# The Fourier transforms of the second block moved into the weave of its last recurrence heads, and the modulation of layer 1 dealt out at an even rate

## The chip, the cores and the metric

One core of one Trainium2 chip runs the whole program. The metric is the time on the device in microseconds (us), the median of several executions. Lower is better.

## The reference, cut to what matters

Two blocks run one after the other over 512 tokens of width 1024. The change touches the second block alone. It has two layers. Layer 0 also carries 256 context tokens beside the 512 (six tiles of 128 tokens), layer 1 has outputs for the 512 alone (four tiles). In each layer a projection `hl @ w_in` is cut into five pieces for a gated recurrence with four heads, q, k and v for a differential attention with four heads, and 256 columns `u` for a Fourier mix:

```python
def fourier_mix(u):
    uh = split_heads(u, FT_GROUPS).astype(jnp.float32)
    y = jnp.fft.fft2(uh, axes=(1, 3), norm="ortho").real
    return y.reshape(u.shape).astype(u.dtype)

yl = jnp.concatenate([hgrn_out(ol_f + ol_b, pl[2]), diff_out(od_l), fourier_mix(pl[8])], axis=-1) @ w_out
ml = modulation(c, w_mod[l], b_mod[l])      # silu(c) @ w_mod: 1024 x 6144, needed when layer l starts
```

The result of the Fourier mix is read only by the output projection (`@ w_out`), after the recurrence. The modulation of layer 1 is read only when layer 1 begins.

## The kernel before

The kernel is written as a plan. Python code adds steps with `P.add(kind, ...)`, and each engine's program then walks the same list and issues its own part of every step, so the order of the plan is the order of every engine's queue. Nothing is reordered on the chip. A step's waits are semaphore values that the plan has worked out. `fence()` makes all engines drain and wait for each other.

TensorE (PE) multiplies, ScalarE (ACT) and VectorE (DVE) copy out of PSUM and do the elementwise work, GpSimd (POOL) helps out, SyncE (SP) issues the loads. In this block projections that must be exact are made of three products of split halves (`SplitWeights.by_token`, `HD` high and `LT`/`LX` low halves of the activations).

The order in each layer `l` of the second block:

1. Token-major projections for q and k with weights `W1` (`tok_split`), rotary embedding, and turns into `QKT`.
2. Six tiles with weights `W2` (columns 3072 to 3584): `DV` (values of the attention) and `U` (input of the transforms), 24 matmuls for each tile.
3. A fence.
4. `rj` / `rj_d`: six additions that join high and low halves into `HT3`, three on POOL (L3240) and three on DVE (L3149). Then `swap`: four copies by POOL's DMA queue (L3244) into `QS` and `KS`, which lie over the low halves and so wait for all six additions.
5. The transforms, bare: tables `k_dft` (2 x 1 MB, both layers) and `k_dftc` (2 x 256 KB, layer 0 alone) are loaded into the two weight slots, multiplied with `U` into `PQ`, and `PQ` is multiplied with the constant `cs64` into `FTT`.
6. A fence, then `attention_stage`, into which the projections of heads 0 and 1 (`project(0)`, `project(1)`) are woven by the rate `FILL`. `project(0)` opens with a load of three weight pieces and waits for it.
7. A fence, then the recurrence. For head `h` in 0 to 3, `main(h)` has 24 lead steps in layer 0 and 16 in layer 1. Into them are woven the modulation of layer 1 (in layer 0 alone, `MODS[h]` steps for each lead step), `flow` (the projections of heads 2 and 3, `FLOW[l]` steps for each lead step: 0.64 and 0.93), and `prepare` of the next head (`RATE`). `modulation` has 24 chunks of 1 MB of weights, 32 `mod_m` matmuls each, one load slot for most of them; each group of four chunks has 32 steps, and one more step opens it, 193 in all. What is left of it after the four heads runs at the end, bare.
8. A fence, then the output projection and the feed-forward layer.

The weave is a counter: `with_some(lead, other, rate)` takes `rate` steps of `other` for each step of `lead`.

```python
for h in range(4):
    lead = main(h) if h < 3 else first_half(main(h))
    together(with_some(with_some(lead, mods, MODS[h]), flow, FLOW[l]), preps[h], RATE[l][h], 1)
```

A matmul group of the weave, `proj`, is added in two halves (`pj0`, `pj1`). With `hold=True` its copy out of PSUM is added later, by `proj_copies`.

## Time and profile before

| what | us |
|---|---|
| time, median of 3 runs | 3159.25 (3156.93 to 3161.83) |
| span of the profiled execution | 3152.5 |
| median less span | 6.8 |
| TensorE busy | 2894.6, 92% of the span |
| VectorE busy | 1617.8, 51% |
| ScalarE busy | 1033.2, 33% |
| GpSimd busy | 192.1, 6% |

The profile is of one execution, of which only the span is listed and no whole time of its own; the 6.8 us between its span and the median of the runs is taken as the part that lies around the span. "PE" is the matmul row, "PEld" its weight loads, "PEclk" the clock that was granted to TensorE as a share of 2.4 GHz. A busy time of PE at a clock under 1.00 is longer than the same work at full clock.

### The profile page before, as it was taken

Reading aid. Unit: us, or ns where it says so; the run is one execution under the profiler, and the core shown is the slowest. Engines: PE = TensorE matmul, PEld = TensorE weight load, DVE = VectorE, ACT = ScalarE, POOL = GpSimd, SP = SyncE. Lnnn points to the kernel's source line nnn. Section 1 sums busy time; section 2 is a strip of 40 time slices with the busy share of each in tenths; the row PEclk is TensorE's granted clock in tenths of the full one; section 3 lists DMA queues with packets and bytes.
Section 4 is the critical chain, followed back from the end, with each engine's and each line's share of the span. In section 5 each row is a group of like instructions: output and inputs, shape, how many; then the busy total and the mean of one; then the engine's idle time right before and its main releaser. Section 6 shows DMA issues by size and latency. Waiting matters only on the chain.

```text
span 3152.5 us, 44843 instructions
## 1 busy us (share of the span) xinstructions
PE 2894.6 (92%) x18762; PEld 2379.0 (75%) x18762; DVE 1617.8 (51%) x3363; ACT 1033.2 (33%) x2010; POOL 192.1 (6%) x240
## 2 busy tenths in 40 slices
PE   7988899999999999898799999999899897899998
PEld 6766688888976666687668888888666687578886
DVE  4333544444446355877763424333935677654444
ACT  3223333223344145344232212111415444332222
POOL 0000000000000100100000000000210245100001
PEclk9999999999999999899899999999999898999999
DMA  7434322222222210222512122121121110223231
GB/s 238 154 107 146 103 74 61 54 59 69 61 101 95 77 34 1 85 81 82 190 65 94 47 74 67 54 67 54 54 72 34 31 41 1 94 94 110 91 105 56
DMA packets 228404, 250.58 MB, mean 79 GB/s; under 512 B 5696, under 2 KB 193196, under 8 KB 226668
## 3 DMA queue, kind: packets, MB, share of 16 engines
q1 hardware_dynamic: 227296, 245.77, 24.4%
q8 instruction: 148, 2.42, 0.3%
q0 software_dynamic: 576, 1.84, 0.3%
q14 instruction: 52, 0.43, 0.0%
q10 hardware_dynamic: 332, 0.12, 0.0%
HBM read 236.43 MB, written 9.44 MB: 78 GB/s over the span
## 4 chain that ended last, share of the span: by engine, by line
PE 55%; DVE 8%; ACT 4%; issue 2%; DMA 1%; POOL 1%; POOLq 0%; SPq 0%; ACTq 0%; DVEq 0%
PE PS L2199 52%; PE PS L2203 2%; ACT AR L181 1%; ACT L176 1%; PE PS L2409 1%; DMA WR<-in_w_in 1%; DVE AR L3181 1%; ACT EX L181 1%; DVE AR L2922 0%; DVE EX L3168 0%; DVE AR L2938 0%; DMA WR<-in_w_mod 0%; ACT STAT L181 0%; POOL HT L3240 0%; DVE AR L2947 0%
## 5 line engine op out<-in xcount | busy, mean ns | idle before, releaser
L2199 PE MATMUL PS<-HI,WC 128*128 128x512 f32 (+2 forms) x1600 | 427.9, 353 | 0.6 <-DVE WC L3162 0.6
L2199 PE MATMUL PS<-AR 128*64 128x64 f32 (+7 forms) x3436 | 301.7, 269 | 63.1 <-ACT AR L181 25.0
L2199 PE MATMUL PS<-DW,DH 128*128 128x384 f32 (+1 forms) x1344 | 357.2, 348 | 0.9 <-DVE AR L2783 0.9
L181 ACT ACTIVATE AR<-PS 128x256 f32<-128x256 f32 (+4 forms) x389 | 165.8, 453 | 553.7 <-PE PS L2199 434.0
L2199 PEld LDWEIGHTS PS<-AR 128*64 128x64 f32 (+5 forms) x3436 | 253.7, 171 | 109.5 <-issue 33.8
L2199 PEld LDWEIGHTS PS<-HI,WC 128*128 128x128 f32 x1600 | 284.0, 189 | 42.5 <-DVE WC L3162 1.1
L2199 PE MATMUL PS<-LO,WC 128*128 128x512 f32 (+2 forms) x800 | 282.2, 353 | 0.0
L2199 PE MATMUL PS<-WR,HT 128*128 128x128 f32 (+2 forms) x1296 | 255.2, 355 | 11.6 <-ACT AR L181 5.8
L2199 PE MATMUL PS<-HT,WR 128*128 128x256 f32 (+1 forms) x928 | 257.2, 429 | 6.7 <-DMA WR<-in_w_in 3.1
L2199 PEld LDWEIGHTS PS<-DW,DH 128*128 128x128 f32 x1344 | 241.9, 192 | 9.7 <-issue 7.1
L2199 PEld LDWEIGHTS PS<-WR,HT 128*128 128x128 f32 x1296 | 193.9, 198 | 66.2 <-issue 41.7
L181 ACT ACTIVATE EX<-PS 128x256 f32<-128x256 f32 (+2 forms) x158 | 66.6, 430 | 513.7 <-PE PS L2199 513.7
L2199 PE MATMUL PS<-WC,AC 128*128 128x512 f32 x960 | 228.4, 395 | 0.3
L2199 PE MATMUL PS<-DW,DL 128*128 128x384 f32 (+1 forms) x672 | 227.3, 338 | 0.0
L2199 PEld LDWEIGHTS PS<-HT,WR 128*128 128x128 f32 x928 | 171.7, 190 | 69.9 <-issue 43.3
L2199 PEld LDWEIGHTS PS<-WC,AC 128*128 128x128 f32 x960 | 179.1, 189 | 44.1 <-DVE AR L3181 7.4
L2203 PE MATMUL PS<-CON,AR 128*128 128x128 f32 (+1 forms) x950 | 153.0, 287 | 56.0 <-DVE AR L3129 16.2
L3162 DVE TENSOR_TENSOR WC<-WR,WC 128x1024 fp32r<-128x1024 f32 x96 | 116.3, 1222 | 165.4 <-ACT WC L181 165.4
L181 ACT ACTIVATE WC<-WR 128x1024 fp32r<-128x1024 f32 x96 | 99.9, 1054 | 273.0 <-PE PS L2199 273.0
L2203 PEld LDWEIGHTS PS<-CON,AR 128*128 128x128 f32 (+1 forms) x950 | 117.0, 147 | 93.2 <-issue 51.4
L3168 DVE TENSOR_TENSOR EX<-EX,PS 128x512 f32<-128x512 f32 x66 | 39.2, 594 | 256.7 <-ACT EX L181 256.7
L2199 PEld LDWEIGHTS PS<-LO,WC 128*128 128x128 f32 x800 | 151.3, 189 | 20.4
(458 smaller groups left out, 4948.1 us busy)
## 6 DMA issues: line engine op xcount, KB each, us to landing
WR<-in_w_ffn_in SPq DMA_DIRECT2D x40, 1024.0 KB, 6.4
WR<-in_w_in_b SPq DMA_DIRECT2D x51, 512.0 KB, 6.0
WR<-in_w_mod SPq DMA_DIRECT2D x12, 2048.0 KB, 8.0
WR<-in_w_mod SPq DMA_DIRECT2D x24, 1024.0 KB, 5.5
WR<-in_w_ffn_out SPq DMA_DIRECT2D x22, 1024.0 KB, 4.9
WR<-in_w_in SPq DMA_DIRECT2D x40, 512.0 KB, 5.3
WR<-in_w_out SPq DMA_DIRECT2D x8, 2048.0 KB, 11.3
WR<-in_w_in SPq DMA_DIRECT2D x4, 2048.0 KB, 7.8
```

Of the source, the lines that this page charges most:

```text
L176: self.o.preload_act_table_set(need)
L181: return self.o.activation(out, in_, func, **kw)
L2199: mm = lambda o, l, r, start, stop: e.o.matmul(o, l, r, start=start, stop=stop, skip_group_check=True)
L2203: m = e.o.transpose(bk[0:a.shape[1], 128 * i:128 * i + a.shape[0]], a, ident[0:a.shape[0], 0:a.shape[0]])
L2409: m = e.o.matmul(o, q, k, start=True, stop=True)
L3162: tt(lo, src, hi.bitcast(F32), ALU.subtract).then_inc(sem("cv_d"))
L3168: tt(v, v, pu, ALU.mult).then_inc(sem("gt_m"))
L3181: tt(y, y, bk, ALU.add).then_inc(sem("dn_d"))
```

## The change

The transforms leave their place between the two projections and the attention. `U` is no longer a buffer: its tiles are written into `FTT`, where the results later replace them. A generator `transform()` does the same products and is the last link of `flow`, behind `project(3)`. It waits in the plan until head 1 has ended, since its tables and `PQ` lie in buffers of head 1 (`X`, `XC`), and copies out on ScalarE alone, one group late. The tables are loaded by `tables()`: for `k_dft` one load of 1792 KB and one of 256 KB, for `k_dftc` one of 512 KB.

The first fence goes. The additions `rj` are all on VectorE, one behind each tile of step 2, 1024 elements a partition as before. The load of `project(0)`'s first three weight pieces is issued behind tile 1 of step 2. Two steps of `project(0)` run ahead of the attention stage, whose count starts one lower. `MODS` goes from (1.4, 1.4, 2.2, 2.6) to (2, 2, 2.2, 2.2). What is left of `flow` after the heads runs at the end like the modulation.

```diff
-        RATE, FILL, MODS = ((1, 2, 2, 1), (1.4, 2.5, 2.5, 1)), ((0.45, 0.58), (0, 0.82)), (1.4, 1.4, 2.2, 2.6)
+        RATE, FILL, MODS = ((1, 2, 2, 1), (1.4, 2.5, 2.5, 1)), ((0.45, 0.58), (0, 0.82)), (2, 2, 2.2, 2.2)
...
-                both_parts = [(DV[:, i, :], 0, 256), (U[:, i, :], 256, 512)][:2 if i < nt else 1]
-                tok_split(i, W2, 512 if i < nt else 256, th, both_parts, eng_of(i))
+                o = [(DV[:, i, :], bk_cols(0, 256)), (FTT[:, :, 128 * i:128 * i + 128], bk_cols(256, 512, 2))][:2 if i < nt else 1]
+                p = tok_split(i, W2, 512 if i < nt else 256, th, o, eng_of(i))
+                cols = slice(128 * i, 128 * i + 128)
+                other = LTs[l][:, :, cols] if i < 4 else LXs[l][:, :, 128 * (i - 4):128 * (i - 4) + 128]
+                P.add("rj", HT3[:, :, cols], HDs[l][:, :, cols].bitcast(F32), other.bitcast(F32), [("pj", p.n)])
...
+                if i == 1:
+                    w = load([(128 * j, 128, w2[:, c:c + 128]) for j, c in enumerate((1536, 2048, 0))], 8, 384)
+                    first_w = [Chunk(w.slot, w.view[:, :, 128 * j:128 * j + 128], w.ready, w.until, ()) for j in range(3)]
...
-            fence()
-            for ks in (slice(0, 4), slice(4, 8)):
-                for lo, other in ((0, LTs[l][:, ks, 0:256]), (256, LTs[l][:, ks, 256:512]), (512, LXs[l][:, ks, :])):
-                    P.add("rj_d" if lo == 256 or (lo == 512 and ks.start) else "rj", HT3[:, ks, lo:lo + 256], HDs[l][:, ks, lo:lo + 256].bitcast(F32), other.bitcast(F32), need)
...
-                tabs = [load_flat(A[name][:, c * kt * n:(c + 1) * kt * n], kt * n) for c in range(2)]
-                ready = []
-                for c in range(2):
-                    v = k3(tabs[c].view, kt)
-                    for f in range(2):
-                        j, bk, until = lring.take()
-                        p = proj_now(bk[:, 0:n], [(U[:, tiles0 + k, 128 * f:128 * f + 128], v[:, k, :]) for k in range(kt)], tabs[c], [], until,
-                                     [(eng_of(f), PQ[:, c, f, 0:n], bk[:, 0:n], None)], pq_until)
...
+            def transform(ring=hturn, heads=heads, set_until=set_until, both=both, FTT=FTT):
+                while not heads[1].ended:
+                    yield
...
+                def one(n, pairs, w, need, to, free):
+                    settle()
+                    while ring.full():
+                        yield
+                    j, bk, b_until = ring.take()
+                    points = []
+                    for p in proj(bk[:, 0:n], pairs, w, need, b_until, [("a", to, bk[:, 0:n], None)], free, hold=True):
+                        if n == 512:
+                            yield
+                    owed.append((j, p, points))
+                    yield
+                    return points
...
+                w = tables("k_dft", [X[:, 0:3584], XC[:, 0:512]], until)
...
+                    for f in range(2):
+                        ready = []
+                        for c in range(2):
+                            pairs = [(FTT[:, f, off + 128 * k:off + 128 * k + 128], rows[kt * c + k]) for k in range(kt)]
+                            ready.append((yield from one(n, pairs, w, [], PQ[c][:, 0:n], free)))
+                        stage_one = (("pj", P.count["pj1"]),)
+                        settle()
+                        yield
+                        yield from one(n, [(cs64[:, 128 * c:128 * c + 128], PQ[c][:, 0:n]) for c in range(2)], None, ready[0] + ready[1],
+                                       FTT[:, f, off:off + n], ())
...
-            due = [0]
+            due = [-1]
+            for _ in range(2):
+                next(filling)
...
-            flow = itertools.chain(*[project(h, prr=hturn, slots=by_quarter, after=heads[0] if h == 3 else None) for h in (2, 3)])
+            flow = itertools.chain(*[project(h, prr=hturn, slots=by_quarter, after=heads[0] if h == 3 else None) for h in (2, 3)], transform())
...
-            for _ in mods:
+            for _ in itertools.chain(mods, flow):
                 pass
```

## Rows read from the trace of the kernel before

**Rows 1.** The page: busy time, share of the span and instructions of two engines.
```profile
PE 2894.6 (92%) x18762; PEld 2379.0 (75%) x18762; DVE 1617.8 (51%) x3363; ACT 1033.2 (33%) x2010; POOL 192.1 (6%) x240
```

**Rows 2.** Stretches: length, busy us of PE, PEld, DVE, ACT, POOL, PEclk, DMA.
```profile
1034.00:1057.00 23.00, 22.93 (x102) 18.66 (x100) 1.51 (x4) 1.35 (x5) 0.00 (x0) 1.00 0.00 1
...
1057.00:1082.80 25.80, 23.13 (x68) 11.95 (x68) 11.06 (x9) 3.57 (x8) 12.47 (x7) 1.00 0.50 137
2315.20:2336.20 21.00, 17.67 (x40) 7.44 (x40) 9.78 (x6) 2.10 (x4) 12.34 (x7) 1.00 0.77 192
```

**Rows 3.** The chain that ended last, layer 0: start us, us, what.
```profile
1049.91 7.04 PE PS L2199 x31
...
1079.07 6.39 DMA WR<-in_w_in
...
1085.51 3.70 PE PS L2199 x8
```

**Rows 4.** The same chain, layer 1.
```profile
2299.82 15.28 PE PS L2199 x90
...
2327.67 8.51 POOLq L3194
```

**Rows 5.** Matmuls of the transform of 512 tokens, layer 0: busy us, mean ns.
```profile
L2199 PE MATMUL PS<-WR,AR 128*128 128x512 f32 x32 | 14.0, 595 | 0.8 <-ACTq L2478 0.8
L2199 PE MATMUL PS<-AR,CON 128*128 128x512 f32 x8 | 3.7, 601 | 0.9 <-ACT AR L181 0.9
```

**Rows 6.** Additions on DVE, duration ns min/median/max.
```profile
L3149 DVE TENSOR_TENSOR HT<-HD,LT x4: 1226/2296/3367, 1057.7 to 2316.7; 128x1024 f32<-128x1024 f32 x4
```

**Rows 7.** The swap's issues on POOL, and POOL's drain behind them, each layer.
```profile
1068.00 2.51 POOL L3244 DMA_DIRECT2D AR<-AR  x4 [0.31 <-POOL HT L3240]
2325.88 2.38 POOL L3244 DMA_DIRECT2D AR<-AR  x4 [0.30 <-POOL HT L3240]
...
L3194 POOLq DRAIN  x1: 5895/5895/5895, 1069.3 to 1069.3; - x1
...
L3194 POOLq DRAIN  x1: 8946/8946/8946, 2327.2 to 2327.2; - x1
```

**Rows 8.** Timeline: first groups of PE behind the second fence of layer 1.
```profile
2336.22 1.26 PE L2409 MATMUL PS<-AR 32*128 32x384 f32 x8 [2.06 <-POOLq L3194]
2337.41 5.02 PE L2199 MATMUL PS<-HT,WR 128*128 128x512 f32 x8
...
2342.36 0.93 PE L2409 MATMUL PS<-AR 32*128 32x384 f32 x8
```

**Rows 9.** Timeline: the last matmuls of `project(3)` in layer 0.
```profile
1478.61 3.84 PE L2199 MATMUL PS<-WR,HT 128*128 128x128 f32 x32
```

**Rows 10.** Stretches: layer 0's recurrence in three, the end of layer 1's; columns as in 2.
```profile
1285.00:1482.00 197.00, 182.66 (x2270) 162.03 (x2271) 147.79 (x422) 77.66 (x150) 14.28 (x4) 0.97 0.30 93
1482.00:1553.00 71.00, 48.31 (x953) 40.76 (x952) 64.92 (x193) 23.27 (x46) 4.15 (x2) 0.83 0.55 178
1553.00:1573.40 20.40, 14.34 (x245) 11.09 (x245) 6.88 (x17) 3.47 (x18) 0.00 (x0) 0.83 0.38 113
...
2648.00:2704.00 56.00, 33.53 (x487) 29.55 (x485) 45.89 (x106) 18.58 (x42) 29.28 (x52) 0.79 0.21 76
```

**Rows 11.** Modulation matmuls between 1300 and 1482 us, ten chunks of 32.
```profile
L2199 PE MATMUL PS<-WR,MISC 128*2 128x128 f32 x320 | 10.6, 272 | 0.0
```

**Rows 12.** Waits from 1553 to 1573.5 us: who waited for whom, us, times, longest.
```profile
DVE AR L2962 <- ACT STAT L181: 6.0, 1, 6.0
DVE MOD L2864 <- PE PS L2203: 4.8, 2, 4.1
...
PEld PS L2199 <- DMA WR<-in_w_mod: 2.5, 1, 2.5
```

**Rows 13.** The page: loads of 2048 KB, count, size, us to landing.
```profile
WR<-in_w_mod SPq DMA_DIRECT2D x12, 2048.0 KB, 8.0
...
WR<-in_w_out SPq DMA_DIRECT2D x8, 2048.0 KB, 11.3
```

More of the change, by code:

```diff
@@ L380, in load @@
             c = Chunk(slot, v, (f"w{slot}", wloads[slot]), wuntil[slot], loads)
-            P.add("load", c)
-            return c
-        def load_flat(ap, cols):
-            slot = wturn[0] % 2
-            wturn[0] += 1
-            wloads[slot] += 16
-            c = Chunk(slot, wslots[slot][:, 0:cols], (f"w{slot}", wloads[slot]), wuntil[slot], [(wslots[slot][:, 0:cols], ap)])
             P.add("load", c)
@@ L1641, in tok_split @@
                 j, bk, until = lring.take()
-                p = proj_now(bk[:, 0:n], w.by_token(l, i, 0, n), w.ready, need, until, [(eng, o, bk[:, lo:hi], None) for o, lo, hi in to], free)
+                p = proj_now(bk[:, 0:n], w.by_token(l, i, 0, n), w.ready, need, until, [(eng, o, view(bk), None) for o, view in to], free)
                 lring.done(j, *p.done)
@@ new lines, in build @@
+                if i == 1:
+                    w = load([(128 * j, 128, w2[:, c:c + 128]) for j, c in enumerate((1536, 2048, 0))], 8, 384)
+                    first_w = [Chunk(w.slot, w.view[:, :, 128 * j:128 * j + 128], w.ready, w.until, ()) for j in range(3)]
+            th = [("rj", P.count["rj"])]
+            turned = [("qturn_" + e, turn_counts["q" + e]) for e in "ad"]
+            for a in (0, 64):
+                P.add("swap", QS[64 - a:128 - a, :, :], QKT[a:a + 64, 0:2, 0:512], th + turned)
+                P.add("swap", KS[64 - a:128 - a, :, :], QKT[a:a + 64, 2:4, 384:768], th + turned)
@@ L1885, in main, with tables, settle @@
                 yield from recur(heads[h], ended)
+            def tables(name, to, until):
+                wloads["f"] += 16 * len(to)
+                at_, loads = 0, []
+                for a in to:
+                    loads.append((a, A[name][:, at_:at_ + a.shape[1]]))
+                    at_ += a.shape[1]
+                w = Chunk("f", None, ("wf", wloads["f"]), until, loads)
+                P.add("load", w)
+                return w
+            def transform(ring=hturn, heads=heads, set_until=set_until, both=both, FTT=FTT):
+                while not heads[1].ended:
+                    yield
+                until, owed = set_until[1], []
+                def settle():
+                    if owed:
+                        j, p, points = owed.pop()
+                        proj_copies(p)
+                        ring.done(j, *p.done)
+                        points += p.done
+                def one(n, pairs, w, need, to, free):
[10 more added lines that the diff above has]
+                    return points
+                PQ, free = [XC[:, 512:1024], XC[:, 1024:1536]], until
+                w = tables("k_dft", [X[:, 0:3584], XC[:, 0:512]], until)
+                rows = [X[:, 512 * k:512 * k + 512] for k in range(7)] + [XC[:, 0:512]]
+                for name, n, off in (("k_dft", T, 0), ("k_dftc", TC, 512))[:2 if both else 1]:
+                    kt = n // 128
+                    if off:
+                        w, rows = tables(name, [X[:, 0:1024]], stage_one), [X[:, 256 * k:256 * k + 256] for k in range(4)]
+                    for f in range(2):
[8 more added lines that the diff above has]
+                                       FTT[:, f, off:off + n], ())
+                        free = (("pj", P.count["pj1"]),)
+                settle()
@@ L3244, in swap @@
                 e.o.dma_start(to, src).then_inc(sem("swap"), 16)
-            return dict(fence=fence, rj=rj, swap=swap, hp2=hp2, hl1=hl1, hl2=hl2, g2=g2, an=an, dump=dumped(e))
+            return dict(fence=fence, swap=swap, hp2=hp2, hl1=hl1, hl2=hl2, g2=g2, an=an, dump=dumped(e))
         def sp_program(e):
```

37 lines of the change are left out of this document (9 added, 28 removed).

## The prediction, as put on record before the changed kernel was run

> **What bounds the kernel now.** I read the page first. TensorE is busy for 92% of the span and VectorE for 51% [rows 1], so what is taken off TensorE's queue is worth its time wherever nothing else sets the pace, and what is moved costs its time again unless it lands in a gap. So I then asked for stretches: the place that the transforms leave, and the place that they go to.
>
> They leave a stretch of 25.8 us in layer 0 and 21.0 us in layer 1 in which TensorE is busy for 23.1 and 17.7 us [rows 2] and the chain runs over TensorE in layer 0 [rows 3]. In layer 1 it runs over POOL's queue, at the end over 8.51 us of POOL's drain, which ends after TensorE has finished the transforms [rows 4]. So the transforms of layer 1 hide most of a wait that is there without them.
>
> They go to the time behind `project(3)`. Its last group of matmuls starts at 1478.61 and ends at about 1482 in layer 0 [rows 9]; in layer 1 the place is about 2648. Up to there the recurrence of layer 0 is bound by TensorE, busy for 182.7 of 197 us [rows 10]. Behind it TensorE is idle for 22.7 of 71 us and 6.1 of 20.4 us in layer 0, 22.5 of 56 us in layer 1, and VectorE is busy for 64.9 of 71 us and 45.9 of 56 us. There is a gap for TensorE work, but VectorE is the bound beside it with only 6 us to spare in the 71.
>
> **The front, step by step.** Removed from TensorE: in both layers the 14.0 and 3.7 us of the 512 tokens [rows 5], 17.7 us, and in layer 0 those of the context too, with which it is 23.1 us [rows 2]. Today the time from the end of the last `W2` matmul to the first score of the attention is 1082.8 - 1056.95 = 25.8 us in layer 0 [rows 2, 3] and 2336.22 - 2315.10 = 21.1 us in layer 1 [rows 4, 8].
>
> What is late next is the swap. It still waits for all additions, and the fence behind it waits for POOL's drain. The additions of tiles 0 to 4 run on VectorE during step 2, where it is busy for 1.5 us in 23 [rows 2]: with that cover gone they would cost five times 1.2 us a layer, so they cost nothing. The last one is exposed. One such addition took 3.36 us beside POOL's and 1.23 us at the least [rows 6]; POOL has none in the new stage, so I take 1.2 us and keep 3.4 us as the other bound. Then 0.3 us to POOL, 2.5 us of issues, and the drain's end: 1069.3 + 5.9 = 1075.2 is 4.7 us behind the last issue's end at 1070.5 in layer 0, and 2336.1 is 7.9 us behind 2328.3 in layer 1, where three weight loads ran beside it [rows 7]. In the new order those weight loads come earlier (their slot is free when `W1` has been used, before tile 1), and the table loads are gone, so I take 4.7 us. Sum: 1.2 + 0.3 + 2.5 + 4.7, with 0.1 for semaphores, 8.8 us of idle TensorE in each layer; the bounds are 8.8 and, with both worse ends, 14.2 us. No project work can fill it, since the two early steps stand behind the fence. They are eight matmuls of 512 columns, 3.7 us as the group at 1085.51 [rows 3], moved ahead of an attention stage in which TensorE is the fullest engine, so they neither gain nor lose.
>
> The first term is 25.8 - 8.8 = 17.0 us gained in layer 0 and 21.1 - 8.8 = 12.3 us in layer 1. In layer 0 the wait for the first weight load goes too: the load landed at 1079.07 + 6.39 = 1085.46, and the next group began at 1085.51, 1.8 us after the scores of 0.93 us that began at 1082.8 [rows 3, 8]; these 1.8 us are gained. Against it, after the drain in layer 1 TensorE ran its first groups slow, 1.26 us for 0.93 and 5.02 for 3.70 [rows 8, 3]. After an idle of 8.8 us layer 0 will pay those 1.7 us as well, layer 1 pays them already. Front in all: 17.0 + 1.8 - 1.7 + 12.3 = 29.4 us gained.
>
> The Trainium skill has a rule that picks between the two ends for the addition: SBUF — State Buffer, Who interferes with whom, says that a VectorE instruction with two SBUF inputs contends with a GpSimd instruction that reads SBUF, and that the second to issue is blocked for the whole of the first. By it the 1.2 us holds once POOL adds nothing, and without it the exposed wait would be 2.2 us longer a layer, 4.4 us in the sum; the minimum beside the maximum agrees with it.
>
> **The recurrence, step by step.** Counting the yields: `project(2)` and `project(3)` take 18 each in layer 0 and 17 in layer 1, the transforms 22 and 14. At 0.64 a lead step the 36 end at lead step 57 of 96 and the 22 more at 91; at 0.93 the 34 end at step 37 of 64 and the 14 more at 52. Both fit before the loop's end, and the trace has `project(3)` end about there [rows 9].
>
> Modulation: at the new rates layer 0's heads 0 and 1 take 96 steps of it instead of 67.2. These 28.8 steps are 3.6 chunks at 10.6 / 10 = 1.06 us each [rows 11], with their turns some 4.4 us of TensorE work moved into the stretch where it is full to 93%: +4 us. Between 0 (all in its gaps) and 4.4. The three loads more that it brings forward are of 1 MB, in a stretch whose DMA share is 0.30 [rows 10], and cost nothing there.
>
> The tail: today 193 steps meet 182.4, so some eleven run bare at the end, and from 1553 to 1573.4 us TensorE waited for a modulation load, VectorE 4.8 us for a turn of it and 6.0 us for the last output behind it [rows 12]. At 24 x 8.4 = 201.6 the modulation ends four lead steps early. I take 5 us gained, between 0 and the 13.3 us that these three waits sum to.
>
> Tables: 2 MB land in 8.0 to 11.3 us [rows 13], and TensorE's first transform product stands in the plan right behind the load with no step between. SP issues it when the last modulation chunk before it has been used, up to one chunk's period earlier. A chunk is 8 of the 2.2 steps a lead step, 3.6 lead steps of some 2.3 us (71 us for 31), 8.4 us. So TensorE waits for 9.6 less an average 4.2, about 5.4 us, between 0 and 11.3; behind it every later instruction of TensorE's queue waits, the next `multiply` of head 2 among them, and VectorE behind that. Since TensorE idles a third of this stretch, I count 3 us. Modulation loads queued behind the tables come up to 10 us late with a period of 8.4: part of the same bound. In layer 1 SP has nothing before it but head 1's end, three lead steps before, and its table is asked for as soon as that is met; the first product follows it by at least those steps and part of head 2, some 10 us: nothing, up to 1 us. The second table of layer 0 is a quarter of the size and has a pair of `cs64` matmuls and a lead step to land in: nothing.
>
> The Trainium skill, DMA: Bandwidth & Descriptors, Anatomy of one DMA, fits a transfer issued from GpSimd as 2.0 us plus bytes over 436 GB/s, by which 2 MB would take 6.8 us, an estimate. By it the wait would be 2.6 us and its cost 1.5 us, the sum 1.5 us better; the table is issued from SP and modulation loads run beside it, so I stay with the rows, which are slower.
>
> The products themselves: 23.1 us in layer 0 for a gap of some 23 us between lead steps 57 and 91, to which the 4.4 us of modulation and the time at the low clock add. A granted clock of 0.83 over 71 us is 24 us at half speed; if half of them were busy, 6 us come back when the gaps are filled. That makes 33 us of room. In layer 1 17.7 us go into about 17.5 idle and 6 of clock. So TensorE will be some 85 to 90% busy next to a VectorE at 82 to 91%. Each half of a product is 1.8 us in front of the next matmul of the recurrence. Bounds: 0, if always in a wait, and 40.8, if never. The nearest row is the stretch before, where TensorE at 93% and VectorE at 75% ran side by side [rows 10]; here VectorE is fuller, and I take a quarter of the 40.8 as delay: 10 us, 6 in layer 0 and 4 in layer 1. The twelve and six copies on ScalarE of 0.4 to 0.6 us lie in a ScalarE that is busy for a third.
>
> Sum for the recurrence: 4 - 5 + 3 + 6 + 4 = 12 us lost. In all 29.4 - 12 = 17.4 us gained. The profiled span becomes 3152.5 - 17.4 = 3135.1 us, and with the 6.8 us by which the median stands above the span, 3141.9 us.
>
> **Rivals.** First, all hidden: the products and tables fall into waits, the recurrence loses 4 us or less or gains by the tail. 29.4 less 4 to plus 5 gives 3125 to 3134 us. For it speak 22.7 and 22.5 us of idle at a low clock; against it VectorE's 64.9 of 71. Second, no change: VectorE and TensorE lock step, half of the 40.8 us is exposed (20 instead of 10), the table wait costs its full 11 and the front's idle is 12 us twice (6 more); 17.4 - 10 - 8 - 6 is a loss of 7 us if all three come and a gain of up to 6 if two do: 3153 to 3165 us. For it speaks that TensorE already waits for VectorE in step and the drain took 8.9 us in layer 1. Third, slower: the one mechanism is that the products land on the recurrence's chain, each half in front of a matmul for which VectorE waits. With all 40.8 us exposed the recurrence loses 4 - 5 + 3 + 41 = 43 and the kernel is 14 us slower, about 3173; it turns slower when more than 27.4 us, two thirds of the 40.8, are exposed. Against it stands the spare unit between a multiply and its reduce in `recur`. Fourth, the move is only half made: banks of the turn ring are full, the transforms lag and some run bare behind the last head. Each step so left costs about 1 us (23.1 / 22), and with eight left the gain is 9 us, 3150: the high end of the forecast's own range.
>
> **Chances.** The forecast, 3134 to 3151 us, 0.61, the fourth rival within its upper end; all hidden 0.18; no change 0.13; slower 0.08. A measurement of this kernel can tell 0.2%, 6.3 us, from no change: faster 0.79, the same 0.12, slower 0.09. The range that leaves out no more than two in ten runs from 3128 to 3154 us.
>
> **What the profile after would show.** The front: a gap of TensorE of about 9 us in each layer, ended by POOL's drain, the additions at 1.2 us each on VectorE, and no wait for a weight load behind it. The recurrence: products of 512 columns out of `X` between `project(3)` and about three quarters of head 3; a wait of TensorE for the table in layer 0 alone; a granted clock near 1.00 where it was 0.83 and 0.79. The stretch from the stage's first matmul to the last fence 8 us longer in layer 0 and 4 us in layer 1. The prediction is wrong if POOL's drain takes more than 12 us of the front, or if VectorE's idle time behind `project(3)` grows by more than 20 us.

## The result, and the profile after

The changed kernel takes 3183.64 us (median of 4 runs, 3182.89 to 3185.59), the kernel before 3158.09 us (4 runs). The ratio is 1.0092, with an interval from 1.0076 to 1.0108: **slower, by 25.6 us between the medians, where 17 us less were forecast**. The profiled execution has a span of 3184.0 us, 31.5 us above that of before. Part of that difference is which executions were profiled: where the time of the profiled execution is listed, it lies 1.3 to 1.7 us above its span, so the one of the kernel before, with a span of 3152.5, must have taken about 3154 us, some 4 us less than its median, and the one of the changed kernel took 3185.59, 2 us more than its median. The 6.8 us that the table of before puts around the span are for the most part this.

TensorE's busy time, on the page of the profile of the changed kernel, is 13 us more than in [rows 1] for the same number of instructions:

```profile
PE 2907.9 (91%) x18762; PEld 2381.0 (75%) x18762; DVE 1609.3 (51%) x3360; ACT 1037.0 (33%) x2019; POOL 171.6 (5%) x234
```

**Where the time went.** SP's queue gives marks that every version has: the store of `x_spill`, the load of `k_mask` at the recurrence's start, and the load of `x_spill` at its end. The timeline of SP, the kernel before and then the changed one:

```profile
985.13 0.34 SPq L3269 DMA_DIRECT2D x_spill<-X  x1
...
1285.30 0.82 SPq L3269 DMA_DIRECT2D AR<-k_mask  x2
1573.34 0.34 SPq L3269 DMA_DIRECT2D X<-x_spill  x1
```

```profile
989.46 0.34 SPq L3297 DMA_DIRECT2D x_spill<-X  x1
...
1283.83 0.81 SPq L3297 DMA_DIRECT2D AR<-k_mask  x2
1604.62 0.34 SPq L3297 DMA_DIRECT2D X<-x_spill  x1
```

Differences of such marks give the stages, in us. "Front" is steps 1 and 2 and the attention, "rec" the recurrence, "other" all that lies outside these four, where the change edits nothing. Each row is of one execution. "Other" differs by up to 14 us between versions with no edit there, so I take the stages as the evidence.

| kernel | front, layer 0 | rec, layer 0 | front, layer 1 | rec, layer 1 | other | span |
|---|---|---|---|---|---|---|
| before | 300.2 | 288.0 | 239.6 | 197.8 | 2126.9 | 3152.5 |
| changed | 294.4 | 320.8 | 231.7 | 199.2 | 2138.0 | 3184.0 |
| mods_alone | 300.3 | 296.0 | 238.0 | 199.0 | 2135.2 | 3168.4 |
| mods_old | 299.0 | 308.5 | 231.8 | 199.2 | 2131.1 | 3169.5 |
| layer0_in_place | 303.5 | 287.0 | 231.6 | 199.0 | 2130.4 | 3151.6 |
| early_tables | 294.4 | 298.6 | 234.3 | 199.2 | 2133.7 | 3160.2 |
| early_old | 294.5 | 290.9 | 231.6 | 199.1 | 2132.6 | 3148.6 |
| no_transforms | 298.8 | 286.5 | 231.6 | 199.0 | 2131.4 | 3147.3 |
| early_first_mod | 298.7 | 309.4 | 231.6 | 198.9 | 2141.3 | 3179.9 |
| first_product_later | 297.1 | 312.0 | 231.5 | 199.1 | 2134.6 | 3174.2 |
| old_rates_half_step | 295.9 | 292.0 | 231.8 | 199.1 | 2135.4 | 3154.2 |
| early_old_swap_sp | 286.6 | 289.5 | 224.6 | 196.2 | 2134.2 | 3131.0 |
| before_swap_sp | 300.1 | 287.4 | 240.1 | 200.0 | 2128.9 | 3156.4 |
| changed_swap_sp | 286.6 | 314.9 | 220.5 | 199.7 | 2130.9 | 3152.5 |
| swap_sp_no_early_steps | 283.0 | 291.7 | 227.3 | 199.5 | 2133.0 | 3134.5 |
| tables_no_early_steps | 286.3 | 289.6 | 229.8 | 198.5 | 2135.2 | 3139.4 |

The changed kernel against before: fronts 5.8 and 8.0 us shorter (29.4 was the forecast for both), recurrence of layer 0 longer by 32.8 us (forecast: 8), of layer 1 by 1.4 (forecast: 4), and 11.1 us outside. So the loss is for the most part one stage: layer 0's recurrence.

How far is a stage to be trusted? In layer 1's front the versions with the same instructions there agree within 0.4 us, early_tables apart (2.6 us more). In layer 0's front they do not. From the attention's first score to the load of `k_mask`, the stretch takes 201.8 or 201.9 us in changed, early_tables and early_old, and 206.2 to 206.4 us in mods_old, no_transforms, early_first_mod, first_product_later, early_old_swap_sp and changed_swap_sp, with 203.3 in old_rates_half_step between them, though the same instructions stand in it. The granted clock takes another course: in the third and the fourth 20 us from the first score it is 0.91 and 1.00 in early_old, 0.99 and 0.84 in no_transforms. What sets the course is not shown. So a difference of up to 4.6 us in this front proves nothing, and the changed kernel's 5.8 us there were measured in the shorter course. In the recurrences the same plan comes out within 2.2 us in layer 0 (early_old, early_old_swap_sp, swap_sp_no_early_steps, tables_no_early_steps), with one exception, changed against changed_swap_sp, 5.9 us.

**The front.** Timeline of the changed kernel on VectorE, POOL and TensorE, with POOL's drain at the fence, first in layer 0, then in layer 1; these answer to [rows 3, 4, 6 to 8]:

```profile
1061.33 1.23 DVE L3181 TENSOR_TENSOR HT<-HD,LX 128x1024 f32<-128x1024 f32 x1 [3.55 <-PE PS L2231]
1063.15 2.51 POOL L3272 DMA_DIRECT2D AR<-AR  x4 [788.30 <-DVEq L2797]
L3226 POOLq DRAIN  x1: 7374/7374/7374, 1064.5 to 1064.5; - x1
1071.93 10.12 PE L2231 MATMUL PS<-HT,WR 128*128 128x512 f32 x16 [10.64 <-POOLq L3226]
1081.98 0.93 PE L2441 MATMUL PS<-AR 32*128 32x384 f32 x8
...
L3226 POOLq DRAIN  x1: 7570/7570/7570, 2349.7 to 2349.7; - x1
2357.33 9.13 PE L2231 MATMUL PS<-HT,WR 128*128 128x512 f32 x16 [10.53 <-POOLq L3226]
2366.39 0.93 PE L2441 MATMUL PS<-AR 32*128 32x384 f32 x8
```

The addition takes the 1.23 us that was forecast. The drain ends at 1064.5 + 7.4 = 1071.9, 6.2 us behind the last issue's end (1065.66), not 4.7. TensorE waits 10.6 us in each layer. Then the two early project steps run: 16 matmuls, not eight, and at a granted clock of 0.70 and 0.78 they take 10.1 and 9.1 us. The first score starts at 1081.98, 20.7 us behind the last `W2` matmul's end at 1061.3, where before it was 25.8.

**The recurrence of layer 0.** Timeline of the changed kernel, SP's queue and then TensorE's, around the two table loads:

```profile
1487.36 7.14 SPq L3292 DMA_DIRECT2D WR<-in_w_mod  x2
1494.61 0.56 SPq L3292 DMA_DIRECT2D X<-k_dft  x1
1495.21 0.43 SPq L3292 DMA_DIRECT2D XC<-k_dft  x1
...
1563.24 8.17 SPq L3292 DMA_DIRECT2D WR<-in_w_mod  x2
1571.45 0.92 SPq L3292 DMA_DIRECT2D X<-k_dftc  x1
```

```profile
1493.01 1.05 PE L2231 MATMUL PS<-WR,MISC 128*2 128x128 f32 x32
1504.36 5.52 PE L2231 MATMUL PS<-X,AR 128*128 128x512 f32 x8 [10.29 <-DMA XC<-k_dft]
...
1569.92 1.05 PE L2231 MATMUL PS<-WR,MISC 128*2 128x128 f32 x32
1577.55 3.78 PE L2231 MATMUL PS<-X,AR 128*128 128x256 f32 x8 [6.58 <-DMA X<-k_dftc]
```

Read them across. TensorE ends a modulation chunk at 1494.06; that frees the slot for which SP's second modulation load has stood waiting; SP issues it, then the table at 1494.61; and the table's product is the very next thing in TensorE's queue. The table gets no lead, and TensorE waits for its whole transfer, 10.3 us: both parts landed 9.1 us behind their issue, within the 8.0 to 11.3 us of [rows 13]. At 1571.45 the same thing happens to the small table, 6.6 us. The products that free its buffer had ended at 1554.7, so it was not they that held its load. The Trainium skill, DMA: Bandwidth & Descriptors, Anatomy of one DMA, says that a semaphore wait of a DMA happens on the issuing sequencer before dispatch; this case's trace agrees: each table was issued within 0.6 us of the end of the chunk that the load ahead of it had waited for.

**Stretches.** The changed kernel, columns as in [rows 2], with [rows 2 and 10] as the counterparts; the last line lies as far behind the load of `k_mask` of layer 1 as the last of [rows 10] does:

```profile
1061.30:1082.80 21.50, 10.87 (x24) 4.33 (x24) 1.23 (x1) 1.26 (x3) 2.51 (x4) 0.68 0.38 91
1285.00:1482.00 197.00, 179.67 (x2279) 158.47 (x2277) 143.52 (x415) 75.53 (x144) 14.28 (x4) 0.95 0.36 109
1482.00:1553.00 71.00, 54.27 (x720) 37.88 (x719) 45.66 (x124) 22.52 (x47) 4.14 (x2) 0.88 0.36 122
...
2671.80:2727.80 56.00, 46.91 (x525) 32.69 (x523) 44.52 (x103) 20.93 (x46) 29.02 (x52) 0.94 0.21 76
```

In layer 1 the products raise TensorE from 33.5 to 46.9 us busy and the clock from 0.79 to 0.94. In layer 0 VectorE, busy for 64.9 of these 71 us before, has 45.7. About half of that is the first table: VectorE's longest wait in the stretch, 10.2 us, is for a product that stands behind the table's, and with the tables early (early_tables) it is busy for 55.0 us. In that stretch of mods_alone it is busy for 58.4 and of early_old for 60.3, so the rates and the products have a part in it too. The second table's wait lies behind this stretch.

### The profile page after: what moved, and what is told of

It is laid out like the page before. It is cut to its first block, busy times and chain, and to the rows that moved or that the text cites. A ratio compares the mean times of both kernels' runs of the same rounds, so it can differ in the third digit from the quotient of the medians.

```text
span 3184.0 us, 44817 instructions
## 1 busy us (share of the span) xinstructions
PE 2907.9 (91%) x18762; PEld 2381.0 (75%) x18762; DVE 1609.3 (51%) x3360; ACT 1037.0 (33%) x2019; POOL 171.6 (5%) x234
## 4 chain that ended last, share of the span: by engine, by line
PE 55%; DVE 8%; ACT 4%; issue 2%; DMA 1%; POOLq 0%; POOL 0%; SPq 0%; DVEq 0%; ACTq 0%
PE PS L2231 52%; PE PS L2235 2%; ACT AR L181 1%; PE PS L2441 1%; ACT L176 1%; DVE AR L3213 1%; DVE STAT L3145 1%; ACT EX L181 1%; DVE EX L3200 0%; POOLq L3226 0%; DMA WR<-in_w_in 0%; ACT STAT L181 0%; DVE AR L2954 0%; DVE AR L3125 0%; DVE OBl L3194 0%
## 5 line engine op out<-in xcount | busy, mean ns | idle before, releaser
L2231 PE MATMUL PS<-AR 128*64 128x64 f32 (+7 forms) x3436 | 299.0, 264 | 52.9 <-ACT AR L181 23.6
L181 ACT ACTIVATE AR<-PS 128x512 f32<-128x512 f32 (+4 forms) x386 | 164.4, 453 | 550.9 <-PE PS L2231 413.1
L2231 PEld LDWEIGHTS PS<-HT,WR 128*128 128x128 f32 x928 | 175.3, 194 | 91.3 <-issue 46.2
L2235 PE MATMUL PS<-CON,AR 128*128 128x128 f32 (+1 forms) x950 | 155.4, 290 | 57.4 <-DVE AR L3161 17.4
```

What stands on the lines that cost most here:

```text
L181: return self.o.activation(out, in_, func, **kw)
L2231: mm = lambda o, l, r, start, stop: e.o.matmul(o, l, r, start=start, stop=stop, skip_group_check=True)
L2235: m = e.o.transpose(bk[0:a.shape[1], 128 * i:128 * i + a.shape[0]], a, ident[0:a.shape[0], 0:a.shape[0]])
```

## The experiments

Each ratio is against the kernel before, measured on the same chip.

**mods_alone: the kernel before with the new rates.**

```diff
-MODS = (1.4, 1.4, 2.2, 2.6)
+MODS = (2, 2, 2.2, 2.2)
```

> The kernel before with only the new rates of the modulation (2, 2, 2.2, 2.2). As forecast, 4 us lost in heads 0 and 1 and 5 us gained at the tail: 3155 to 3160 us. If the 9 us by which the first output of head 2 came later in the changed kernel are all due to the rates, and the tail gives 5 back: 3160 to 3164 us.

Measured: 3168.75 us, ratio 1.0037 (1.0025 to 1.0049), above both expected ranges; the recurrence of layer 0 is 7.9 us longer. One wait stands out in the timelines of VectorE and TensorE, 11 us into the recurrence:

```profile
1297.89 0.48 DVE L2854 MEMSET PS<- 128x512 f32 x1
1298.48 1.88 PE L2199 MATMUL PS<-WR,MISC 128*2 128x128 f32 x32 [7.38 <-issue]
```

With rate 2 the opening step of the modulation and its first product fall into one lead step. The opening step issues the load, at 1288.88 with 8.3 us to landing, and has VectorE clear the bank that the product writes. So TensorE stands first before a load just issued, and then before VectorE, whose clearing comes behind its other work of that lead step and ends at 1298.37, 0.1 us ahead of the product. The profile names no releaser, and no run parts the two. In the kernel before TensorE waited 3.97 us for VectorE in that place, so some 4 us are new:

```profile
1292.94 1.34 PE L2199 MATMUL PS<-AR 128*64 128x64 f32 x20 [3.97 <-DVE AR L2938]
```

VectorE takes the first of its twelve outputs of the recurrence 4.9 us later than before, the tenth 11.8 us later, and the recurrence ends 7.9 us later: the tail does give 3.9 us back, but 11.8 were lost ahead of it.

**mods_old: the changed kernel with the old rates.**

```diff
-MODS = (2, 2, 2.2, 2.2)
+MODS = (1.4, 1.4, 2.2, 2.6)
```

> The changed kernel with the old rates of the modulation (1.4, 1.4, 2.2, 2.6). Theory: of the 32.8 us by which layer 0's recurrence grew, some 9 us come from modulation moved into the stretch where TensorE is full, so this run is 4 to 9 us faster than the changed kernel (3175 to 3180 us; the bare tail of 11 steps comes back). Rival: the tables and products cause it all and the old rates only put the tail back: 3184 us or slower.

Measured: 3170.19 us, ratio 1.0042 (1.0030 to 1.0054). That is 13.5 us below the changed kernel, where 4 to 9 were expected. The recurrence of layer 0 is 12.3 us shorter than in the changed kernel and still 20.4 us longer than before. TensorE waits for both tables as in the changed kernel:

```profile
PE PS L2231 <- DMA XC<-k_dft: 10.3, 1, 10.3
PE PS L2231 <- DMA X<-k_dftc: 6.8, 1, 6.8
```

**early_tables: the changed kernel with the tables loaded ahead of their use.** `k_dft` is asked for in head 2's lead as soon as head 1 has ended, `k_dftc` behind the third product of the first table.

```diff
+def tables_early(steps, ...):
+    for _ in steps:
+        if heads[1].ended and not tab:
+            tab["k_dft"] = tables("k_dft", [X[:, 0:3584], XC[:, 0:512]], set_until[1])
+        yield
...
+lead = main(h) if h < 2 else tables_early(main(h)) if h == 2 else first_half(main(h))
```

> The changed kernel with its table loads placed earlier in the plan: k_dft as soon as head 1 has ended, some six lead steps before the first product, and k_dftc behind the last product that reads the first half of k_dft. Nothing else moves. Theory A: TensorE's two waits for tables (10.3 and 6.6 us) are true losses, since SP's queue holds the load behind a modulation load that waits for the chunk just multiplied; both waits vanish and the time falls by 10 to 17 us, to 3167 to 3174 us. Theory B: the recurrence is bound by the products between its matmuls, and the waits only took the place of others: under 5 us faster, 3179 us or more.

Measured: 3160.88 us, ratio 1.0009 (0.9999 to 1.0018). Theory A holds in kind, and the gain is larger than its range: 22.2 of the 32.8 us are gone from layer 0's recurrence, more than the 16.9 us of the two waits themselves. That is with the new rates; with the old ones (mods_old against early_old, below) the same edit takes off 308.5 - 290.9 = 17.6 us, where the waits were 10.3 and 6.8. Why it is worth 4.6 us more beside the new rates is not shown.

**layer0_in_place: old rates, layer 0's transforms back in their place, layer 1 as changed.**

```diff
-early_w = banks(6, 7), {0: first_w}
+early_w = banks(6, 7), {} if both else {0: first_w}
...
-... for h in (2, 3)], transform())
+... for h in (2, 3)], iter(()) if both else transform())
```

> Old rates of the modulation, layer 0's transforms in their old place (its additions stay on VectorE behind the tiles, its first fence and weight load as before), layer 1 as in the changed kernel. Theory: layer 1 alone gains 8.0 us in front and loses 1.4 us in its recurrence, so 3150 to 3153 us against 3158 before. Rival: what layer 1 gains is given back in the stage behind the recurrence, where the profile after stood 6.3 us longer: 3157 to 3160 us.

Measured: 3156.4 us, ratio 0.9997 (0.9988 to 1.0005), no difference, and between the two expected ranges. Layer 1's half gains 8.0 us in its front and gives 1.3 back in its recurrence. Layer 0's front is 3.3 us longer, 2.7 of them behind the first score, where nothing is edited and the front scatters by more than that; the additions on VectorE, ahead of it, can account for no more than 0.7.

**early_old: early tables and old rates together**, the two edits above.

> Both measured repairs together: the table loads early, and the old rates of the modulation. Early tables alone took 22 us off the changed kernel, the old rates 13 us; in layer 0's recurrence, 298.6 us with early tables, the old rates should take another 8 to 12 us, so 3149 to 3153 us, faster than the kernel before. If the two repairs share a cause (a queue of SP that is less crowded), they overlap: 3156 us or more.

Measured: 3152.34 us, ratio 0.9980 (0.9970 to 0.9990), as expected. With its tables early and its rates old the idea of the change is worth 6 us. No instruction waits for a table any more; the instructions of tile `k_dft` in layer 0 in that trace, with none that waited for them:

```profile
L3302 SPq DMA_DIRECT2D X<-k_dft x1: 341/341/341, 1451.6 to 1451.6; - x1
...
who waited for it (us, times):
busy tenths in 40 slices 0000000000000000000000000000000000000000
DMA to landing us min/median/max: 7.1/7.8/8.6
```

**no_transforms: old rates, the transforms left out altogether.** The output projection then reads the columns untransformed, so this kernel computes something else; its time bounds what the products cost in the recurrence.

```diff
-... for h in (2, 3)], transform())
+... for h in (2, 3)], no_transform())
```

> The changed kernel with the old rates, and with the transforms left out altogether: no table is loaded, no transform product made, and the output projection reads the untransformed columns. It prices the transforms where the change puts them: against early_old the difference is what 40.8 us of TensorE work cost inside the recurrence. As forecast (a quarter exposed): 10 us. If they lie in waits: 0 to 4 us. If in the chain: 20 us or more.

Measured: 3146.06 us, ratio 0.9961 (0.9946 to 0.9976), 6 us below early_old. The same 71 us behind `project(3)`, first in early_old and then in no_transforms, columns as in [rows 2]:

```profile
1475.90:1546.90 71.00, 60.85 (x929) 43.02 (x932) 60.28 (x182) 27.24 (x55) 4.15 (x2) 0.98 0.49 162
```

```profile
1483.70:1554.70 71.00, 48.58 (x957) 41.22 (x957) 65.05 (x193) 23.25 (x46) 4.14 (x2) 0.83 0.55 179
```

12 us more of busy TensorE fit into the stretch, and the clock goes from 0.83 to 0.98. So 40.8 us of products cost 6 us by the medians and 4.4 us in layer 0's recurrence, between the forecast's 10 and nothing. In layer 1 the recurrence takes the same time with them and without them.

**early_first_mod: early tables and new rates, with the first modulation load issued ahead of the loop** and the first product only at the third lead step.

```diff
+if both:
+    next(mods)
...
-with_some(lead, mods, MODS[h])
+with_some(lead, mods, MODS[h], 2 if h == 0 else 0)
```

> Early tables, new rates, but the first modulation load is issued ahead of the loop and its first product stands two lead steps later. In the run with the new rates alone TensorE stood 7.4 us before its first modulation product, which the rate of 2 puts in the same lead step as its load. Theory: this wait, with the low clock behind it, is most of what the rates cost: 5 to 8 us faster than early tables alone, 3153 to 3156 us. Rival: the cost is TensorE work moved into full heads, and the first wait only stands in for others: 3159 us or more.

Measured: 3174.43 us, ratio 1.0053 (1.0038 to 1.0068), 13.5 us *slower* than early_tables: the expectation fell. The 7.3 us wait went, with both the load and the clearing of the bank ahead of the loop, and head 0's first output came 2.0 us earlier in the recurrence, as expected. But by the fourth it was 8.4 us later. All later modulation pieces had shifted against the projections, and a weight load of a projection came late behind modulation loads in SP's queue. TensorE's waits around that place, in mods_alone and in early_first_mod (early_tables has 2.0 us there):

```profile
PE PS L2199 <- DMA WR<-in_w_in: 3.1, 1, 3.1
```

```profile
PE PS L2243 <- DMA WR<-in_w_in: 5.4, 1, 5.4
```

In the kernel before that wait is 0.8 us.

**first_product_later: early tables and new rates, the count started half a lead step lower.**

```diff
-with_some(lead, mods, MODS[h])
+with_some(lead, mods, MODS[h], 0.5 if h == 0 else 0)
```

> Early tables and the new rates (3160.9), the modulation's count started half a lead step lower, so that its first load and its first product no longer fall in the same lead step; everything else in it comes at most half a lead step later. Theory: of the 8 us that the rates cost, about 4 are TensorE's 7.3 us wait for that first load, in place of the 4.0 us it waits for VectorE anyway, and the rest is a projection weight load behind a modulation load in SP's queue. So 3156 to 3158 us. Rival (any shift of the order moves a projection's weight load further behind, as with the first load ahead of the loop, where that wait grew to 5.4 us): 3161 to 3174. Second rival (the cost is the TensorE time that was moved, 2 us a head, not a wait): 3160 to 3161.

Measured: 3172.43 us, ratio 1.0046 (1.0033 to 1.0059). The theory and the second rival fell; the time lies in the first rival's range. Again the first wait went (head 0's first output 3.0 us earlier than in early_tables), and again more was lost behind it: 11.5 us in the median. But the wait for the weight load, which that rival had growing, stayed at the 2.0 us of early_tables, so it is not the cause here. The stretch where the fourth output falls behind, 110 to 130 us into the recurrence, in early_tables and then here:

```profile
1390.26:1410.26 20.00, 17.54 (x185) 14.61 (x185) 14.68 (x30) 9.51 (x19) 4.14 (x2) 1.00 0.32 94
```

```profile
1393.17:1413.17 20.00, 15.58 (x104) 12.48 (x106) 10.04 (x24) 5.74 (x17) 2.08 (x1) 0.83 0.16 43
```

The granted clock drops to 0.83 and 104 matmuls are done where 185 were.

**old_rates_half_step: the same half step, at the old rates.** The same edit as above, on early_old.

> The same kernel as early tables with old rates (3152.3), with the modulation's count started half a lead step lower and nothing else: no rate is changed and no work is added. Theory (what the rates cost is where each modulation piece falls in TensorE's and SP's queues, and this order was tuned by hand): 3155 to 3162 us, the loss in heads 0 to 2. Rival (the cost is the modulation work that the new rates bring into heads 0 and 1, so a mere shift is free): 3151 to 3153.5.

Measured: 3151.84 us, ratio 0.9980 (0.9971 to 0.9989), the same as early_old and in the rival's range. So the general theory that any shift of the modulation's place costs time is wrong: at the old rates a half step costs nothing, at the new ones 11 us. The rival's reason, that a mere shift is free, fails by the same 11 us.

**early_old_swap_sp: early tables, old rates, and the swap's four DMAs issued by SP instead of POOL.** SP has no drain in the fence.

```diff
-            return dict(fence=fence, swap=swap, hp2=hp2, ...      # POOL
+            return dict(fence=fence, hp2=hp2, ...
...
-            return dict(begin=begin, ..., stored=stored)           # SP
+            return dict(begin=begin, ..., stored=stored, swap=swap)
```

> As early_old, with the four swap copies issued by SP in place of POOL's queue, so that the fence waits for no drain of POOL. Theory: TensorE's idle of 10.6 us in front is POOL's issues and drain; it falls to 2 to 3 us and the two project steps run while the copies fly: up to 7 us less in each layer's front, 3137 to 3143 us, unless the first scores then wait for the copies (about 3 us each: 3143 to 3147 us).

Measured: 3132.3 us, ratio 0.9911 (0.9897 to 0.9925), 25.1 us below the kernel before by the medians and 20.0 below early_old, 5 us more than expected. TensorE's first group behind the fence in early_old, then here, then SP's issue:

```profile
1067.09 10.20 PE L2241 MATMUL PS<-HT,WR 128*128 128x512 f32 x16 [10.77 <-POOLq L3236]
```

```profile
1060.66 7.10 PE L2241 MATMUL PS<-HT,WR 128*128 128x512 f32 x16 [1.41 <-DVEq L2807]
```

```profile
1060.54 3.10 SPq L3319 DMA_DIRECT2D AR<-AR  x4
```

The wait is 1.4 instead of 10.8 us, and the group runs at the full clock: 7.1 us for the same 16 matmuls that took 10.2 in early_old. The landing of the swap now lies under these 7.1 us. Two things changed with the issuer. POOL has no drain to make behind copies, and the copies landed 3.7 and 4.1 us behind their issue, against 6.0 and 6.2 in the changed kernel with POOL as the issuer; the issuing itself took longer, 3.1 us for 2.5. The Trainium skill, DMA: Bandwidth & Descriptors, Issuing engine by pattern, puts simple loads and stores on Sync (SP here) and says that what Sync and ScalarE issue is generally faster; by the time to landing the trace agrees, by the time to issue it does not.

**before_swap_sp: the kernel before with the swap on SP**, behind the transforms (`P.add("swap", ...)` moved to just ahead of the second fence, and the handler moved as above).

> The kernel before, with only the four swap DMAs issued by SP, behind the transforms and ahead of the fence. Theory (what costs in the front is POOL's drain where nothing else covers it): TensorE waited for the drain 2.1 us in layer 1 and not at all in layer 0, where the transforms cover it. So 0 to 4 us are gained, 3154 to 3158 us. Rival (a DMA that POOL issues costs the attention about 10 us a layer wherever it stands): 3138 us, 20 less. The case in which the change is worth nothing even with a good swap is this kernel at 3132.

Measured: 3160.24 us, ratio 1.0005 (0.9996 to 1.0014), no difference, 2 us above the theory's range and far from the rival's 3138. Where the transforms cover the drain, moving the swap gains nothing that can be measured. So the gain of early_old_swap_sp needs both: transforms elsewhere, and no drain in their place.

**changed_swap_sp: the changed kernel with the swap on SP and nothing else.**

> The changed kernel with nothing but the swap on SP; the late tables and the new rates stay. Theory: the drain's wait and the recurrence's losses are separate terms and add up, so the same 20.0 us as between the two kernels with early tables and old rates come off: 3183.6 - 20.0 = 3164 us, between 3160 and 3167, and the front is short by 8 us in layer 0 and 7 in layer 1. Rival (the fence's wait hides part of the recurrence's loads or clock, so that they don't add): 3170 or more.

Measured: 3155.88 us, ratio 0.9995 (0.9983 to 1.0006): 28 us below the changed kernel, where 20 were expected and 17 to 24 allowed. The fronts are 7.8 and 11.1 us shorter, as the theory had it in layer 0 and more in layer 1. 5.9 us are gone from layer 0's recurrence too, though TensorE still waits 10.2 and 6.4 us for the tables; that part I can't explain, and it is more than the same recurrence varies by elsewhere.

**swap_sp_no_early_steps: early_old_swap_sp without the two early project steps.**

```diff
-due = [-1]
-for _ in range(2):
-    next(filling)
+due = [0]
```

> The fastest kernel so far (3132.3) without the two project steps ahead of the attention. The prediction's step (early steps neither gain nor lose): 3132, within 2. Theory from the trace: layer 1 gives the 7.4 us back (no change there), layer 0 does not, since the stretch from the first score to the recurrence's start was 202.5 us with the two steps inside and 201.9 without. So without them layer 0's front is 6 to 7 us shorter in all: 3125 to 3127 us.

Measured: 3128.8 us, ratio 0.9910 (0.9896 to 0.9924), against 0.9911 with them: no difference, and between the two expectations. In both layers TensorE now waits for the landing of the swap; its waits in layer 0's front:

```profile
PE PS L2449 <- DMA AR<-AR: 8.1, 1, 8.1
```

The 7.1 us of steps had covered those 8.1, so here the test says nothing on whether the steps are given back.

**tables_no_early_steps: the same edit on early_old**, where POOL's drain covers the landing.

> Early tables and old rates with the swap on POOL (3152.3), without the two project steps ahead of the attention. With the swap on SP this test said little, since the early steps cover the landing of the swap there (TensorE waited 8.1 us for it without them). Here POOL's drain covers that landing. The prediction's step (neither gain nor lose): 3152, within 2. Theory (layer 1 gives the 7.4 us back, layer 0 does not): front of layer 0 shorter by 6 to 7, 3146 us. The 0.6 to 3.5 us that the run with the swap on SP gained would stand between: 3149 to 3151.

Measured: 3134.85 us, ratio 0.9925 (0.9910 to 0.9939), 17.0 us below old_rates_half_step, which was run beside it, and further than any theory had said. By the profiles it is 9.2 us below early_old and 14.8 below old_rates_half_step. The first score and the start of the recurrence, TensorE's and SP's timeline:

```profile
1067.86 1.66 PE L2449 MATMUL PS<-AR 32*128 32x384 f32 x8 [10.56 <-POOLq L3234]
```

```profile
1271.80 0.82 SPq L3305 DMA_DIRECT2D AR<-k_mask  x2
```

The drain is still waited for in full. Counted from the stage's first mark, the first score comes 10 us earlier, and layer 0's front ends 8.2 us earlier than in early_old (9.6 than in old_rates_half_step). So the early steps were a loss in layer 0, for most of their 10.2 us, and of 1.7 to 1.9 us in layer 1. These two make 10 to 11.5 us; the medians have 17, and the rest is not shown.

## Why the prediction was wrong

**"Front in all: 29.4 us gained": 13.8.** Two terms were mis-sized. The idle was 10.6 us a layer instead of 8.8, the drain ending 6.2 us behind the last issue instead of 4.7; that is 3.6 us. The larger one is the step on the two early project steps, "eight matmuls of 512 columns, 3.7 us ... so they neither gain nor lose". They are 16 matmuls, 10.1 and 9.1 us at the low clock that follows the wait (0.70 and 0.78). The group of eight at 1085.51 is one step, and two run ahead. In layer 0 the attention gave almost nothing back: from the first score to the recurrence it took 1283.8 - 1082.0 = 201.8 us, with the steps inside 1285.3 - 1082.8 = 202.5. Idle 1.8 and steps 10.1 less 0.7 make 11.2 of the 11.3 us that layer 0's front fell short of 17.1; that it closes so well is luck, since this stretch took 4.5 us longer in other versions. In none of them was more given back. tables_no_early_steps shows the same by taking them out. In layer 1, 6.4 of 9.1 us were given back. That TensorE is the fullest engine of a stage does not mean that work taken out of it shortens the stage.

**Tables: "I count 3 us", "the second table ... nothing": 18 to 22.** The bound was right (10.3 us against "between 0 and 11.3"), the choice within it was wrong. It took an average lead of half a chunk's period. But the load stands in SP's queue behind a modulation load that waits for the chunk that TensorE has just used, so whatever the period, the lead is zero; the small table's wait of 6.6 us, which the sum left out, comes the same way. Taken away together they gave back 17.6 us at the old rates (mods_old to early_old), for 17.1 us of bare waits, and 22.2 at the new ones (changed to early_tables), for 16.9. So the waits cost at least their length, and the discount to three fifths for a TensorE that "idles a third of this stretch" was wrong. VectorE stopped for 10.2 us behind the first table, so it did not run on beside the wait as that discount supposes.

**Modulation: "+4" and "-5 us in the tail": +7.9.** The new rates cost 7.9 us in mods_alone, 7.7 us between early_old and early_tables, and 12.3 us with the late tables. About 4 us are the first product in the lead step of its own load and of the clearing of its bank, which the yields would have told. In the tail 3.9 us came back, near the 5 forecast; it is the +4 that failed, with 11.8 us lost by the tenth output. What the rest of that is stays open: the theory of a projection's load held up in SP's queue covers 3.4 us of the loss in early_first_mod (5.4 for 2.0 in early_tables) and nothing in first_product_later (2.0 us), and the theory that any shift costs fell with old_rates_half_step. early_first_mod and first_product_later show that at the new rates the place of the pieces is worth 11 to 13 us; why it is worth nothing at the old ones, I can't say.

**Products: "10 us, 6 in layer 0 and 4 in layer 1": 4.** 2.8 and 1.3 us in early_old against before; 6 us by the medians of early_old and no_transforms. The step was right in kind and too dear: the granted clock rose with them, from 0.83 to 0.98, and in layer 1 from 0.79 to 0.94; how much of the difference the clock paid was not measured by itself. The rival on the slower side put everything on these products and needed 27.4 us of them; the kernel is slower through waits that are not theirs. The fourth rival did not come true either: in the changed kernel the last transform product of layer 0 ends at 1596.7, ahead of the last output at 1603.9, so none ran bare. In the second rival, "a gain of up to 6 if two do" is a slip: 17.4 less the two smallest terms, 6 and 8, is 3.4.

**The sum.** Layer 0's recurrence: 22.2 for the tables (changed to early_tables), 7.7 for the rates (early_tables to early_old) and 2.8 for the products (early_old to before) make its 32.8 us. They must, since each is the step from one kernel to the next; taken in the other order the rates are 12.3 and the tables 17.6. What stands by itself is that the rates alone cost 7.9 us in the kernel before. Against the forecast, the fronts are 15.6 us short of their 29.4, and the two recurrences lose 34.2 us where 12 were counted. With 1.4 in layer 1 and 13.8 gained in the fronts, the edited stages lose 20.4 us; the other 11.1 us of the profiled span lie where nothing was edited. About 6 of them are the choice of executions, since the medians differ by 25.6 us and the spans by 31.5; why the rest comes is not shown. Of the two conditions named for a wrong prediction, the drain stayed below 12 us, and VectorE's idle time grew by 19.3 us in the 71, just under the 20 given and about half of it through the first table. Over all of the time behind `project(3)` it grew by 28 us, from 19.5 of 91.3 to 47.6 of 122.6, so by that reading the sign had come.

## What to carry to other kernels

A load placed on an in-order queue is worth the lead of what stands ahead of it there, not its own: if that waits for the engine that will use the new load next, the lead is zero. Give it its place behind something long done. Before moving cover away from a fence, ask what the cover hid: here a drain of POOL, 5.9 and 8.9 us long before, for which TensorE waited 0 and 2.1 us, and 7.4 and 7.6 us long after, in a wait of 10.6 us a layer; with SP as the issuer the wait was 1.4 us. And count what a stage gives back from its own chain, by taking the work out once, rather than from the busiest engine's share.

## What the runs showed of the hardware that was not expected

A wait of TensorE costs twice: behind 10.3 to 11.3 us of idle the same 16 matmuls took 8.6 to 10.2 us in nine kernels (granted clock 0.70 for 10.1 us), behind 1.4 us of idle 7.1 us at 1.00. And extra work can be nearly free: in 71 us TensorE did 12.3 us more of busy work at a granted clock of 0.98 than without it at 0.83, and the stage grew by 4.4 us. Last, the same instructions of one stage, layer 0's attention, took from 201.8 to 206.4 us in different versions, with the drops of the granted clock in other places.
